# A gated-delta mixer: three output-weight remainders move into the inverse's last level, solved columns go ahead of a silu, the gates' products go between blocks

## The reference, cut to what matters

```python
def gated_deltanet(x, w_in, conv_w, a_log, dt_bias, norm_w, w_out):
    p = x @ w_in
    qkv, z, b, a = jnp.split(p, ...)
    qkv = jax.nn.silu(causal_depthwise_conv(qkv, conv_w))
    q, k, v = jnp.split(qkv, ...)                # 8 heads of 128
    q = l2_normalize(q) * GDN_DK ** -0.5
    k = l2_normalize(k)
    beta = jax.nn.sigmoid(b)
    g = -jnp.exp(a_log) * jax.nn.softplus(a + dt_bias)
    o = chunk_gated_delta_rule(q, k, v, beta, g)
    o = gated_rms_norm(o, z, norm_w)
    return o.reshape(B, T, GDN_VAL) @ w_out

def chunk_gated_delta_rule(q, k, v, beta, g):
    G = jnp.cumsum(g, axis=-1)
    decay = jnp.exp(jnp.where(incl, G[..., :, None] - G[..., None, :], -jnp.inf))
    L = jnp.where(strict, jnp.einsum('bhncd,bhnsd->bhncs', k * beta, k) * decay, 0.0)
    sol = triangular_solve(L + I, [v * beta, k * beta * exp(G)])   # per chunk and head
    ...                                          # recurrence over the chunks
```

## Time and profile before

| | us |
|---|---|
| median of 3 runs | 2466.81 |
| runs | 2469.43, 2459.6, 2466.81 |
| profiled execution | 2464.71 |
| its span, first to last instruction | 2462.9 |
| TensorE busy | 2408.8 |
| VectorE busy | 1760.4 |
| ScalarE busy | 1175.4 |

### The profile page before, as it was taken

One profiled execution on the slowest core, in us unless ns is written; L12 is line 12 of the kernel. 1 busy time (PEld: TensorE's weight loads), 2 busy tenths in 40 slices (PEclk: granted clock), 3 DMA queues, 4 the chain that ended last, 5 costly groups with the idle time before them and its releaser, 6 DMA issues.

```text
span 2462.9 us, 47920 instructions
## 1 busy us (share of the span) xinstructions
PE 2408.8 (98%) x18258; PEld 2230.0 (91%) x18258; DVE 1760.4 (71%) x2908; ACT 1175.4 (48%) x1819; POOL 75.8 (3%) x149
## 2 busy tenths in 40 slices
PE   8999999999999999989999999999999999989998
PEld 6877877778988999988999998999989999988998
DVE  5788799988847876786666868665567667776665
ACT  5454522233645444566444555444545446466444
POOL 1000000000000000000300000000000000000000
PEclk9999999999999999999999999999999999999999
DMA  8433355554524565422655522555424554322653
GB/s 315 158 108 128 112 181 194 180 181 157 178 90 145 195 183 169 131 92 70 197 182 184 178 88 78 196 182 186 147 87 161 187 174 162 110 87 80 202 175 133
DMA packets 119708, 378.20 MB, mean 154 GB/s; under 512 B 11655, under 2 KB 29063, under 8 KB 119184
## 3 DMA queue, kind: packets, MB, share of 16 engines
q1 hardware_dynamic: 107040, 328.62, 40.6%
q0 software_dynamic: 12528, 47.62, 5.8%
HBM read 375.15 MB, written 1.05 MB: 153 GB/s over the span
## 4 chain that ended last, share of the span: by engine, by line
PE 78%; DVE 11%; issue 6%; ACT 3%; DMA 1%; DVEq 1%; SPq 0%; ACTq 0%
PE gb L608 20%; PE gb L610 19%; PE gb L609 19%; DVE w_lo L577 2%; PE mb L3010 2%; PE mb L717 1%; DVE W L1627 1%; PE mb L608 1%; PE mb L609 1%; PE mb L610 1%; DVE W L2738 1%; PE gb L2991 1%; DMA X<-in_x 1%; ACT w_hi L569 1%; DVE W L1251 1%
## 5 line engine op out<-in xcount | busy, mean ns | idle before, releaser
L608 PE MATMUL gb<-Xs,w_hi 128*128 128x256 f32 (+1 forms) x3422 | 1037.5, 303 | 10.2 <-DVE w_lo L577 4.9
L610 PE MATMUL gb<-Xs,w_lo 128*128 128x256 f32 (+1 forms) x3422 | 1022.0, 299 | 0.0
L609 PE MATMUL gb<-Xs,w_hi 128*128 128x256 f32 (+1 forms) x3336 | 993.2, 298 | 0.0
L569 ACT ACTIVATE w_hi<-raw 128x1024 fp32r<-128x1024 f32 x582 | 610.6, 1057 | 691.4 <-PE gb L610 650.9
L577 DVE TENSOR_TENSOR w_lo<-raw,w_hi 128x1024 fp32r<-128x1024 f32 x582 | 705.9, 1223 | 210.8 <-ACT w_hi L569 203.8
L608 PEld LDWEIGHTS gb<-Xs,w_hi 128*128 128x128 f32 x3422 | 644.8, 188 | 57.8 <-issue 17.5
L610 PEld LDWEIGHTS gb<-Xs,w_lo 128*128 128x128 f32 x3422 | 645.2, 189 | 26.0
L609 PEld LDWEIGHTS gb<-Xs,w_hi 128*128 128x128 f32 x3336 | 629.3, 189 | 23.4 <-issue 1.9
L609 PE MATMUL gb<-Fs,w_hi 128*128 128x256 f32 (+1 forms) x966 | 278.2, 288 | 0.0
L608 PE MATMUL gb<-Fs,w_hi 128*128 128x256 f32 (+1 forms) x880 | 248.9, 283 | 0.7 <-ACT Pj L1776 0.7
L610 PE MATMUL gb<-Fs,w_lo 128*128 128x256 f32 (+1 forms) x880 | 247.1, 281 | 0.0
(11 more groups left out here) (469 smaller groups left out, 3287.2 us busy)
## 6 DMA issues: line engine op xcount, KB each, us to landing
raw<-in_up SPq DMA_DIRECT2D x264, 512.0 KB, 3.3
raw<-in_down SPq DMA_DIRECT2D x96, 512.0 KB, 3.7
R<-in_mod_later POOLq DMA_DIRECT2D x80, 512.0 KB, 3.6
raw<-in_gdn_in SPq DMA_DIRECT2D x64, 512.0 KB, 3.3
raw<-in_down SPq DMA_DIRECT2D x48, 384.0 KB, 4.0
raw<-in_hgrn_in SPq DMA_DIRECT2D x32, 512.0 KB, 4.2
raw<-in_ev_in SPq DMA_DIRECT2D x24, 512.0 KB, 4.2
raw<-in_gla_in SPq DMA_DIRECT2D x24, 512.0 KB, 4.0
```

The lines of the kernel that those rows point to most:

```text
L569: nc.scalar.activation(hi, raw[:, slot, 0:hi.shape[1]] if len(hi.shape) == 3 else like(raw[:, slot], hi), ACT.Identity).then_inc(*hi_ready ...
L608: nc.tensor.matmul(to, weight_block(w_slot, 0, k), x_hi, start=start, stop=False)
L609: nc.tensor.matmul(to, weight_block(w_slot, 0, k), x_lo, start=False, stop=False)
L610: return nc.tensor.matmul(to, weight_block(w_slot, 1, k), x_hi, start=False, stop=stop)
```

## The change

In the tile loop VectorE makes no remainder at n = 29, 30 and 31; the three follow the first, second and third of the four copies of the inverse's last level. ScalarE, from tile 28 on, takes the tap of a tile first and splits an output weight after the silu; the fourth of these splits moves to the inverse's step 10. At n = 31 the four `keep_cols` stand before `silu(30)`; `silu(31)` and `keep_keys(0)` move behind ScalarE's first copy in the inverse. The gates' products are done one block at a time between the blocks of tile 4, and write two PSUM banks in place of one.

```diff
+        OUT_LATE = 28
...
+            def gates(k):
+                for t in range(TC):
+                    last = nc.tensor.matmul(mb[:, 1 + t, 0:16], X[:, k, chunk(t)], w_ba[:, i, k, :], start=k == 0, stop=k == KC - 1)
+                if k == KC - 1:
+                    last.then_inc(*pe_a.inc())
+
             pe_group(pe, 0, T, ready)
             for n in range(AHEAD, len(GDN_TILES)):
-                tile(n)
-                if n == 3:
-                    for t in range(TC):
-                        for k in range(KC):
-                            last = nc.tensor.matmul(mb[:, 2, 16 * t:16 * t + 16], X[:, k, chunk(t)], w_ba[:, i, k, :],
-                                                    start=k == 0, stop=k == KC - 1)
-                    last.then_inc(*pe_a.inc())
+                tile(n, gates if n == 4 else None)
...
             for n, (kind, h) in enumerate(GDN_TILES):
-                act_tile(act, 1, wait=True)
+                if n < OUT_LATE:
+                    act_tile(act, 1, wait=True)
+                else:
+                    act.wait_ge(*gemm_out.due("act"))
...
+                    if n == 31:
+                        for g in range(4):
+                            keep_cols(g)
                     if n and GDN_TILES[n - 1][0] != "z":
                         silu(n - 1)
+                    if OUT_LATE <= n < 31:
+                        split_hi(act, ahead["act"].next())
...
-                if n == 31:
-                    keep_cols(0)
-                    keep_cols(1)
-            keep_cols(2)
-            keep_cols(3)
-            silu(31)
             conv_kept.due("act_kept", 16)
-            keep_keys(0)
...
+                if n == 0:
+                    keep_keys(0)
+                    silu(31)
+                if n == 10:
+                    split_hi(act, ahead["act"].next())
...
             for n, (kind, h) in enumerate(GDN_TILES):
-                dve_tile(dve)
+                if n <= OUT_LATE:
+                    dve_tile(dve)
...
                     if l == LEVELS - 1:
                         nc.vector.tensor_copy(pair(inv_T)[HALF[0], :, HALF[1]], made[HALF[0], :, HALF[1]]).then_inc(*inv_done.inc())
+                        if OUT_LATE + 1 + g < len(GDN_TILES):
+                            dve_tile(dve)
                         continue
```

More of the change, by code:

```diff
@@ L2594, in smalls @@
                 nc.scalar.activation(e_small[:, 0, :], vcol("a_log", 8 * i, 8), ACT.Exp)
-                nc.scalar.activation(beta, mb[:, 2, 0:32].rearrange("p (a c) -> p a c", a=2)[:, :, 0:8], ACT.Exp, scale=-1.0)
+                nc.scalar.activation(beta, mb[:, 1:3, 0:8], ACT.Exp, scale=-1.0)
                 nc.scalar.activation(ln_t, ln_t, ACT.Ln, bias=ones[:, 0:1]).then_inc(*smalls_exp.inc())
@@ L2745, in softplus_arg @@
                 dve.wait_ge(*pe_a.due("dve"))
-                ba = mb[:, 2, 0:32].rearrange("p (a c) -> p a c", a=2)
+                ba = mb[:, 1:3, 0:16]
                 dt = vcol("dt_bias", 8 * i, 8).unsqueeze(1).broadcast_to([P, 2, 8])
```

## The result

The changed kernel takes 2482.24 us (median of 6 runs, 2478.0 to 2489.2); the kernel before took 2468.04 beside it (6 runs, 2459.6 to 2471.99). The ratio is 1.0074, with a 95% interval of 1.0055 to 1.0093: **slower by 14 us by the medians and 18 by the ratio, where 7 us less were forecast**. The profiled execution has a span of 2478.8 us against 2462.9, and a mean granted clock of 0.988 against 0.992.

A forecast was written before the change was run, and what follows sets the result against it. VectorE was taken as the limit where input tiles meet the inverse, TensorE paying again through its clock. Stage A -1.9 and B -5.2 gave -7.1 us: 2459.7 on the median of 2466.8, stated as 2459, range 2450 to 2467.

The forecast's parts named there:

- Part 3: Gates' products between the blocks of tile 4: the clock is kept there, minus 1.4 us per stage.
- Rival (b): Clock falls anyway at the joint and in tile 4: 2.9 and 2.8 us come back, about 2465; chance 0.18.
- Part 1: Joint of input tiles and inverse: without three remainders, columns before `silu(30)`, first inverse step starts 3.3 us earlier per stage.
- The clock at the joint: Inverse step 0, behind the input tiles: full clock kept, minus 1.2 us in stage A, minus 1.7 in B.
- Part 2, the copies: Inverse's last level: remainders between the four last copies make TensorE wait longer, plus 2.0 us per stage.
- The clock behind the last level: Products of values and keys behind the inverse: clock falls in both stages, A plus 2.0 us, B minus 0.8.
- Rival (c): Low clock behind the last level through all the chunk recurrence: up to 11 us more per stage, about 2475; chance 0.05.

The follow-up runs named there:

- sum_late: The changed kernel with the key sums of head 0 moved from behind tile 3 to behind tile 4; 2462.09 us, ratio 0.9996 against the kernel before.
- gates3: The changed kernel with the gates' products between the blocks of tile 3 in place of tile 4; 2455.99 us against 2461.91 before, ratio 0.9967.
- p3: The kernel before with only the gates' products put between the blocks of tile 4, and their two readers; 2477.73 us, ratio 1.0062.
- p12: The changed kernel with the gates' products put back in one piece behind tile 3; 2459.72 us against 2461.68 before, ratio 0.9990.
- late_lo: The changed kernel with gates back behind tile 3 and the three remainders moved behind VectorE's two negated copies; 2454.95 us against 2461.91 before, ratio 0.9969.
- gates3_lo: The changed kernel with gates between the blocks of tile 3 and the three remainders behind VectorE's negated copies; 2450.03 us against 2461.91 before, ratio 0.9944.
- gates5: The changed kernel with the gates' products between the blocks of tile 5 in place of tile 4; ratio 1.0027 against the kernel before.

## Why the prediction was wrong, point by point

**Part 3, the step that failed.** "I take the clock as kept" and "The gates' own readers stand behind tile 4 already, so their later end costs nothing": the term of minus 1.4 per stage. The prediction asked who waits for the gates, and not who had been waiting behind them. The key sums, next in TensorE's queue, were ready 0.4 us before the gates ended. The row that carries the 3.5 us was read as a cost to be spread out, and it was a cover. The row taken for the clock (1454.45) was right for what it shows, thin work with no standstill before it; sum_late and gates3 repeat it for the gates between the blocks. It says nothing of thin work behind a standstill. In place of minus 1.4 per stage, a wait of 2.97 us and 17 us at 0.50 made tile 6 9.6 us late in each stage, and part 3 alone cost 16 us (p3). Rival (b) let the clock fall in tile 4, but at the price of the gain alone, 2.8 us for both stages. No rival had the wait or a low stretch of 17 us, which is why the range missed as well.

**Part 1: right.** From the first column transpose to the first inverse step it was 7.38 us and is 4.05, in B too: minus 3.33 per stage, forecast 3.3.

**The clock at the joint: right.** Step 0 at 1.00 and 2.13 us in both stages: minus 1.2 and minus 1.7.

**Part 2, the copies: right.** 4.39 in place of 2.43 us, plus 1.96, forecast 2.0.

**The clock behind the last level: right in kind, too low by 1.2 us in all.** It fell in both stages. A: 6.17 us for the 32 products against 3.67 (1110.77 to 1114.44), plus 2.5 (forecast 2.0). B: 6.38 against 6.48, minus 0.1 (forecast minus 0.8). The estimate that a longer gap takes half of its length out of the low stretch is not borne out: in B nearly all of the products ran low, longer gap or not.

Put together, parts 1 and 2 as read in the trace after are -0.1 us in A (-3.33 - 1.24 + 1.96 + 2.5) and -3.1 in B (-3.33 - 1.67 + 1.96 - 0.1), where the prediction had -0.5 and -3.8. p12 measured minus 2. So 1 to 2 us of the error are in these parts, and the rest is part 3, as far as the intervals tell. Rival (c), the slower one, had the wrong place for its low clock: the products behind the last level were low for 6 us as in the forecast, not through the recurrence.

## What to carry to other kernels

Before you move work out of a queue, look at what comes next in that queue, and when its inputs arrive by the trace: a busy row with no wait behind it may be covering one, and the wait appears at its full length when the cover goes. Where a standstill of TensorE can't be avoided, put wide products behind it and the thin ones ahead of it: the same 32 thin products cost 16 us behind the wait (the wait included) and gained 6 to 8 us (with parts 1 and 2) in front of it, between the blocks of tile 3. Work that another engine does between links of a chain belongs into that engine's next long idle stretch, which the trace shows by its length (late_lo: 5 us less than p12).

## What the runs showed of the chip

The same interleaved instructions ran at either level of the clock for as long as they lasted: in tile 4, 20 instructions in 2 us at 1.00 (sum_late) and 11 at 0.50 (after), with TensorE busy for 2.00 of 2.00 us in both. What differed was what lay before the tile, 3 us of standing still or work. Behind the standstill the clock fell within 2 us of the first instruction (in after at 971.2 and 2080.5, in p3 at 972.3 and 2078.3), and with the thin products it was low for 17 us in three of these four stages and for 14 in the last. With wide products alone behind the same standstill (gates5) it was low for 3.4 and 6.8 us. A standstill isn't needed for a fall: in stage A of p12 it came inside 32 thin products in one piece, at 971.1. The Trainium skill, "TensorE: Matmul & The Clock Gate", section "What's actually happening", says that the throttled state is the default and that activity releases it. In the row of 2081.00 to 2097.00 TensorE is busy for 16.00 of 16 us and the clock is 0.50 throughout; the busy share alone would not have told the level.

The low clock behind the last level came with a gap of only 0.58 us as well, in six stages (B of before and p3, both of late_lo and of gates3_lo; the mean clock over 5.5 us was 0.69 in stage A of late_lo), and did not come in stage A of before and of p3. What decides between them was not settled.
